# Loading the context tokens after the modulation weights in a two-block kernel, and turning their tiles between the first two products

## The chip, the core and the metric

The kernel runs on one core of one Trainium2 chip. The core has five engines with an instruction queue of their own: TensorE (PE, matrix products and transposes), VectorE (DVE), ScalarE (ACT), GpSimd (POOL) and SyncE (SP, which here issues every DMA). They run side by side and wait for each other through semaphores. The metric is the device time of one execution in microseconds, lower is better; the median of the runs is compared.

## What is computed

Two transformer blocks run on 512 latent tokens of width 1024. The first one also reads 256 context tokens. Only its beginning matters here:

```python
def modulate(h, g, shift, scale):
    return rmsnorm(h, g) * (1 + scale) + shift

sh_a, sc_a, g_a, sh_f, sc_f, g_f = modulation(c, ada_w[l], ada_b[l])              # silu(c) @ ada_w + ada_b
csh_a, csc_a, ... = modulation(c_ctx[None, :], ada_w[l], ada_b[l])
y_lat, y_ctx = token_mixer(modulate(x, norm1_g[l], sh_a, sc_a), modulate(h_ctx, norm1_g[l], csh_a, csc_a), w_in[l], ...)
```

`token_mixer` multiplies both sets of tokens by `w_in` and goes on with a gated recurrence in 8 heads, a convolution and attention. Then come a mixture of experts and the second block. All of it is in float32.

## The kernel before

Tokens stand along the free axis in the main buffers, so that the tokens, which arrive with 128 of them on the partitions, must first be turned. `HT` holds both kinds turned: columns 0 to 255 (`0:C`) are the context, columns 256 to 767 (`C:T`) the latent tokens, in KC = 8 chunks of 128 features. There are NT = 6 tiles of 128 tokens: t = 0 to 3 (LT = 4) are latent, t = 4 and 5 context.

**Start-up.** SP issues, in this order: the head of the constants, the four latent tiles, the context (L340, one transfer of 1 MB), 13 small rows of vectors (`rows1`), two of the eight units of modulation weights (phase `mod`, 1 MB each, of `ada_w`), 7 more rows (`rows2`), and the other six units. Then follow the eight units of `w_in` for head 0 (phase `hg`, 0.5 MB each), which lie over the places of modulation units 4 to 7, so that their issue waits until PE has used these. Behind them SP runs `sp_late_first` (L347 and on): the rest of the constants, then a wait for `turn_out` = 6 (all six tiles turned, since the token buffers are reused) and the first three "late" pieces.

ACT norms one tile after the other (`act_unit_tile`, four instructions and a half-row of small ones). PE turns each (L364, 8 transposes into two banks of PSUM, waits `x_unit`), DVE copies it to `HT` (L387). In `pe_setup` the turning of tiles 2 to 5 alternates with the products of modulation units 0 to 3 (L444); units 4 to 7 come after it. After unit 7, DVE copies the sums (L512), PE turns them (L504), and DVE makes shift and scale from them (L519, L527).

**The first norm.** `dve_first` (L633) applies shift and scale to the latent chunks (8 instructions 512 wide), then to the context's chunks (8 instructions 256 wide), and then builds `ht_sums` from the latent columns: for four pairs of chunks the sums and differences (L1881, L1883, L1885) that the seven-product scheme of later products wants.

**Head 0 on PE** (`pe_hg`): plain product 0 and plain product 1 over the latent tokens (L719, 8 chunks each, banks 0 and 1), the gates over the context (L745, bank 4), a wait for `ht_sums`, the product group 1 ("quad 1", L1863, 28 matrix products), values (L760), quad 2 (L1863), values, and the query (L768). The quads wait for `hq_out`, which says that DVE has taken the previous result out of the banks. A profile counts each of these float32 products twice.

**The late pieces on DVE** (`dve_hg`). The other two thirds of the modulation weights are multiplied on DVE in 32 pieces of 0.5 MB (L479, L481). Three buffers hold them; SP issues piece m when piece m - 3 is used (L469). DVE's order is: `dve_first`; `dve_hg_quad` 0 and the convolution (L825 to L832) which need plain products 0 and 1; pieces 0 to 8; quad 1 out of its banks (L1895 to L1902); pieces 9 to 17; quad 2 out of its banks; pieces 18 to 24; `dve_begin` (L861, L862), for which PE's first step of head 1 (L851) waits.

POOL forms sums of weights (`weight_sums`, L1870 to L1875), first when units 2 and 3 of `w_in` have arrived.

Of the kernel before, what the change touches and what calls it, by code (L numbers as in the profile page):

```python
# [13 lines left out]
KC = D // P  # L14
# [3 lines left out]
LT, CT_ = S // P, C // P  # L18
NT = T // P
# [81 lines left out]
def wait(eng, sem, n):  # L101

    if not (isinstance(n, int) and n <= 0):
        eng.wait_ge(sem, n)
# [83 lines left out]
def mixed_block_kernel(nc, A, out):  # L188

    ctx = ExitStack()  # L190
    with ctx:
        sems = {}

        def sem(name):
            if name not in sems:
                sems[name] = ctx.enter_context(nc.semaphore(name))
            return sems[name]
# [18 lines left out]
        psum = ctx.enter_context(nc.psum_tensor("psum", [P, 8, BANK], F32))  # L216
# [95 lines left out]
        def sp_rows(sp, rows, plan, full):  # L312

            r = n = 0
            for name, k in plan:
                if k == 0:
                    for half in range(2):
                        sp.dma_start(rows[r:r + 1, 64 * half:64 * half + 64], A[name]).then_inc(full, 16)
                        n += 1
                    r += 1  # L320
                    continue
                flat = A[name]
                if name in ("c_ctx", "final_norm_g", "final_norm_g_2"):
                    src = flat.rearrange("(r n) -> r n", n=P)
                elif name in ("conv_w", "conv_w_2"):
                    src = flat[0].rearrange("t (r n) -> (t r) n", n=P)
                else:
                    src = flat.rearrange("l (r n) -> (l r) n", n=P)
                sp.dma_start(rows[r:r + k, :], src).then_inc(full, 16)
                n += 1  # L330
                r += k
            return n
# [3 lines left out]
        def sp_setup(sp):  # L336
            sp.dma_start(consts[:, 0:CONST_HEAD], A["const_table"][:, 0:CONST_HEAD]).then_inc(sem("consts_in"), 16)
            for t in range(LT):
                sp.dma_start(x_tok[:, t, :], A["x"][0].rearrange("(t p) d -> t p d", p=P)[t]).then_inc(sem(f"x_in_{t}"), 16)
            sp.dma_start(c_tok, A["ctx"][0].rearrange("(t p) d -> p t d", p=P)).then_inc(sem("ctx_in"), 16)  # L340
            assert sp_rows(sp, rows1, ROWS1, sem("rows1_in")) == N_ROWS1

        def sp_setup_late(sp):
            assert sp_rows(sp, rows2, ROWS2, sem("rows2_in")) == N_ROWS2
# [9 lines left out]
                eng.wait_ge(sem("ctx_in"), 16)  # L354

        def turn_bank(n):
            return psum[:, 2 * (n % 2):2 * (n % 2) + 2, :].rearrange("p b n -> p (b n)")

        def pe_turn_tile(pe, t):

            pe.wait_ge(sem("x_unit"), t + 1)
            wait(pe, sem("turn_out"), t - 1)
            for k in range(KC):
                mm = pe.transpose(turn_bank(t)[:, k * P:(k + 1) * P], x_unit[:, t, k * P:(k + 1) * P], ident)  # L364
            mm.then_inc(sem("turned"), 1)

        def pe_setup(pe):
            pe.wait_ge(sem("consts_in"), 16)
            pe.wait_ge(sem("rows1_in"), 16 * N_ROWS1)
            pe.transpose(psum[:, 7, 0:123], rows1[0:123, :], ident[0:123, 0:123]).then_inc(once("rows1_turned"), 1)  # L370
            pe_turn_tile(pe, 0)
            pe_turn_tile(pe, 1)
            pe.wait_ge(sem("rows2_in"), 16 * N_ROWS2)
            pe.wait_ge(sem("vectors"), 1)
            pe.transpose(psum[:, 7, 128:128 + 92], rows2[0:92, :], ident[0:92, 0:92]).then_inc(once("rows_turned"), 1)
            for t in range(2, NT):
                pe_turn_tile(pe, t)
                pe_mod_first(pe, t - 2)
            for k in range(NT - 2, KC):
                pe_mod_first(pe, k)  # L380
            pe_mod_turn(pe, 0)

# [6 lines left out]
        def dve_setup(dve):  # L389
            dve.memset(psum[:, 4:7, :], 0.0)  # L390
            dve.drain()
            await_once(dve, "rows1_turned")
            dve.tensor_copy(vec1[:, 0:123], psum[:, 7, 0:123])
            dve.drain()
            dve.sem_inc(sem("vectors"), 1)
            dve_turn_tile(dve, 0)
            await_once(dve, "c_exp")
            dve.tensor_scalar(c_exp, c_exp, 1.0, None, ALU.add)
            dve.drain()
            dve.reciprocal(c_exp, c_exp)  # L400
            dve.drain()
            dve.tensor_tensor(silu_c.rearrange("p k w -> p w k"), c_exp.rearrange("p (w k) -> p w k", w=2),
                              vec1[:, CVEC:CVEC + 16].rearrange("p (w k) -> p w k", w=2), ALU.mult)\
               .then_inc(once("silu_c"), 1)
            dve_turn_tile(dve, 1)
            await_once(dve, "rows_turned")
            dve.tensor_copy(vec2[:, 0:92], psum[:, 7, 128:128 + 92]).then_inc(sem("vectors"), 1)
            for t in range(2, NT):
                dve_turn_tile(dve, t)

        def act_unit_tile(act, t):
# [217 lines left out]
        def dve_first(dve):  # L629

            for w, at_, end in ((0, C, T), (1, 0, C)):
                for k in range(KC):
                    dve.tensor_scalar(HT[:, k, at_:end], HT[:, k, at_:end], scale1[:, k, w:w + 1],  # L633
                                      mod[:, SH_A * KC + k, w:w + 1], ALU.mult, ALU.add).then_inc(sem("first_normed"), 1)
            dve.drain()
            for q in range(KC // 2):
                token_sums(dve, HT[:, 2 * q:2 * q + 2, C:T], ht_t[:, q])
            dve.sem_inc(once("ht_sums"), 1)
# [333 lines left out]
        def pe_hg(pe):  # L972

            pe_hg_plain(pe, 0)
            pe_hg_plain(pe, 1)
            pe_hg_gates(pe, 0, lambda: None)
            await_once(pe, "ht_sums")
            pe_hg_quad(pe, 0, 1, None)
            pe_hg_values(pe, 0, 0)
            pe_hg_quad(pe, 0, 2, None)  # L980
            pe_hg_values(pe, 0, 1)
            pe_hg_query(pe, 0)
            pe.wait_ge(sem("head_values_out"), 2)
            pe.wait_ge(sem("consts_in"), 32)
            pe_hg_head(pe, 1)
            pe_hg_head(pe, 2, True)
            with pe.Fori(3, HEADS) as i:
                pe_hg_head(pe, i)
# [2450 lines left out]
        PE_STEPS = [pe_setup, pe_hg, pe_tail, pe_attn, pe_merge, pe_router, pe_experts, pe_mix_norm, pe_in2, pe_dn, pe_wout2, pe_xproj, pe_xattn, pe_xo, pe_mlp, pe_last]  # L3439
        DVE_STEPS = [dve_setup, dve_mod, dve_first, dve_hg, dve_tail, dve_attn, dve_merge, dve_router, dve_experts, N(dve_norm, n_mix), dve_in2, dve_dn, dve_wout2, dve_norm_x, dve_xq, dve_xattn, dve_xo, dve_mlp, dve_last]  # L3440
        ACT_STEPS = [act_setup, act_hg, act_tail, act_attn, act_merge, act_router, act_experts, act_mix_norm, act_in2, act_dn, N(act_norm, n_mem), N(act_squares, n_x), act_xproj, act_xattn, act_xo, act_mlp, act_last_root, act_last]
        BETWEEN = {"mod": {1: sp_setup_late}, "hg": LATE_BETWEEN, "merge": {3: sp_x_again}, "experts": {SLOTS.index(0) - 1: sp_await_w_out}}
        SP_STEPS = [sp_setup] + [lambda e, n=n: ws.load(e, n, BETWEEN.get(n, {}), 3 if n == "hg" else 1) for n in ws.phases]
        SP_STEPS.insert(5, sp_router)
        SP_STEPS.insert(1 + 1 + 1 + list(ws.phases).index('pool2'), sp_small2)
# [56 lines left out]
```

## Time and profile before

| | us |
|---|---|
| median of 3 runs | 2726.17 |
| lowest, highest | 2725.04, 2728.87 |
| the profiled execution | 2727.93 |
| its span in the trace | 2726.2 |
| PE busy | 2648.6 |
| DVE busy | 1347.0 |
| ACT busy | 559.9 |

The trace covers the span; some 1.7 us of the execution lie outside it. PE is busy in 97% of the span, so what can be won lies in the few stretches where it stands. A digit of the profile's 40 slices stands for 68 us, and only the first slice shows PE well under full, with DMA at nine tenths. All times below are microseconds from the start of the span.

### The profile page before, as it was taken

To read this page: it belongs to the slowest core of one execution; us is meant where nothing else is said; L and a number is where in the kernel's file an instruction comes from. 1 tells how busy PE (TensorE), PEld (TensorE's weight loads), DVE (VectorE), ACT (ScalarE), POOL (GpSimd) and SP (SyncE) were. 2 spreads that over 40 slices of the span, in tenths; PEclk is the share of its full clock that TensorE was granted. 3 is DMA by queue.
4 is the path that set the end of the run, shared out by engine and by line. 5 is a ranking of instruction groups with operands and counts; after the bars stand their busy time and mean duration, and the time that the engine had idled before them with its cause. 6 is when DMAs were issued, how large, how long until landed. Compare 5 with 4: busy or idle time off the path is not lost.

```text
span 2726.2 us, 32908 instructions
## 1 busy us (share of the span) xinstructions
PE 2648.6 (97%) x12972; PEld 1868.0 (69%) x12972; DVE 1347.0 (49%) x2449; ACT 559.9 (21%) x942; POOL 177.3 (7%) x140
## 2 busy tenths in 40 slices
PE   6999999999999999998999999999999999999998
PEld 4788888888666666885433333334595877888887
DVE  5775566655555666545111111156472345654654
ACT  3122121222343343311111111132322112000001
POOL 1222221220000000231000000000000000000000
PEclk9999999999999999999999999999999999999999
DMA  9722221211112111336799999942003421323331
GB/s 337 224 81 59 55 58 42 62 31 39 47 55 55 50 52 47 93 94 240 284 409 409 409 409 409 409 126 70 24 1 93 139 62 47 92 79 93 87 84 47
DMA packets 332313, 374.79 MB, mean 137 GB/s; under 512 B 11329, under 2 KB 274326, under 8 KB 330902
## 3 DMA queue, kind: packets, MB, share of 16 engines
q1 hardware_dynamic: 331910, 371.93, 40.4%
q8 instruction: 90, 1.47, 0.2%
q10 hardware_dynamic: 272, 1.05, 0.1%
q14 instruction: 41, 0.34, 0.0%
HBM read 370.85 MB, written 2.10 MB: 137 GB/s over the span
## 4 chain that ended last, share of the span: by engine, by line
PE 89%; DVE 5%; DMA 3%; DVEq 1%; ACT 1%; issue 1%; SPq 0%; ACTq 0%
PE psum L1863 30%; PE psum L2250 12%; PE psum L1543 7%; PE psum L2428 5%; PE psum L760 3%; PE psum L1192 2%; PE psum L2107 2%; PE psum L2152 2%; PE psum L855 2%; PE psum L2966 2%; DMA arena<-in_ada_w 2%; PE psum L745 2%; PE psum L768 2%; PE psum L1399 2%; PE psum L1451 2%; PE psum L1428 2%
## 5 line engine op out<-in xcount | busy, mean ns | idle before, releaser
L1863 PE MATMUL psum<-arena 128*128 128x256 f32 x4144 | 908.0, 378 | 1.8 <-ACT arena L813 0.8
L1863 PEld LDWEIGHTS psum<-arena 128*128 128x128 f32 x4144 | 778.0, 189 | 119.0 <-issue 8.6
L2250 PE MATMUL psum<-arena 128*64 128x512 f32 x1536 | 349.5, 600 | 4.0 <-DMA arena<-in_w_down 2.4
L2250 PEld LDWEIGHTS psum<-arena 128*64 128x64 f32 x1536 | 103.7, 137 | 221.0 <-issue 217.3
L1543 PE MATMUL psum<-arena 128*128 128x256 f32 x896 | 206.6, 381 | 0.1
L1543 PEld LDWEIGHTS psum<-arena 128*128 128x128 f32 x896 | 164.7, 189 | 32.6 <-issue 11.4
L2157 DVE SCALAR_TENSOR_TENSOR arena<-psum,arena 128x512 f32<-128x512 f32 x64 | 48.1, 752 | 233.8 <-PE psum L2152 233.2
L2428 PE MATMUL psum<-arena 128*128 128x512 f32 (+1 forms) x416 | 157.0, 534 | 0.0
L1895 DVE TENSOR_TENSOR arena<-psum,arena 128x256 f32<-128x256 f32 x66 | 28.0, 425 | 260.8 <-ACT arena L1908 184.2
L2428 PEld LDWEIGHTS psum<-arena 128*128 128x128 f32 x416 | 79.7, 192 | 74.9 <-issue 70.6
L1870 POOL TENSOR_TENSOR arena<-arena 128x512 f32<-128x512 f32 x34 | 48.3, 1422 | 1058.2 <-DMA arena<-in_w_in 572.1
L1908 ACT ACTIVATE arena<-psum 128x256 f32<-128x256 f32 x32 | 12.3, 384 | 420.0 <-PE psum L1863 420.0
L760 PE MATMUL psum<-arena 128*128 128x128 f32 x768 | 88.3, 275 | 0.0
L760 PEld LDWEIGHTS psum<-arena 128*128 128x128 f32 x768 | 87.2, 192 | 0.1
L1416 ACT ACTIVATE arena<-psum,arena 128x768 f32<-128x768 f32 x64 | 57.4, 898 | 123.8 <-DVE arena L1410 123.7
L1192 PE MATMUL psum<-arena 128*128 128x512 f32 (+1 forms) x192 | 78.6, 560 | 0.0
L1408 DVE TENSOR_REDUCE arena<-psum 128x1 f32<-128x768 f32 x64 | 61.3, 958 | 23.9 <-PE psum L1399 22.5
L885 DVE TENSOR_TENSOR arena<-arena 128x768 f32<-128x768 f32 (+6 forms) x56 | 25.5, 454 | 95.9 <-PE psum L855 93.4
L2152 PE MATMUL psum<-arena 128*128 128x512 f32 x128 | 69.8, 633 | 0.0
L1438 ACT ACTIVATE arena<-psum 128x768 f32<-128x768 f32 x64 | 49.6, 812 | 98.0 <-PE psum L1428 97.1
L2107 PEld LDWEIGHTS psum<-arena 128*128 128x128 f32 x512 | 60.6, 198 | 12.8 <-issue 11.4
L782 ACT ACTIVATE arena<-psum 128x256 f32<-128x256 f32 x23 | 8.8, 384 | 292.2 <-PE psum L1863 292.2
(411 smaller groups left out, 3378.1 us busy)
## 6 DMA issues: line engine op xcount, KB each, us to landing
arena<-in_w_gate SPq DMA_DIRECT2D x64, 1024.0 KB, 18.5
arena<-in_w_up SPq DMA_DIRECT2D x64, 1024.0 KB, 18.4
arena<-in_w_down SPq DMA_DIRECT2D x64, 1024.0 KB, 18.5
arena<-in_w_in SPq DMA_DIRECT2D x120, 512.0 KB, 4.9
arena<-in_ada_w SPq DMA_DIRECT2D x32, 512.0 KB, 4.8
arena<-in_w_up SPq DMA_DIRECT2D x32, 512.0 KB, 5.4
arena<-in_w_down SPq DMA_DIRECT2D x32, 512.0 KB, 5.2
arena<-in_ada_w SPq DMA_DIRECT2D x8, 1024.0 KB, 13.0
```

The costliest lines, as they stand in the source:

```text
L745: mm = pe.matmul(psum[:, gates_bank(i), d * C:(d + 1) * C], ws.dst("hg", 4 + d)[:, k, :], HT[:, k, 0:C], start=(k == 0), stop=(k == KC - 1))
L760: mm = pe.matmul(psum[:, bank, t * P:(t + 1) * P], HT[:, k, tile * P:(tile + 1) * P], ws.dst("hg", 6)[:, k, :], start=(k == 0), stop=(k == ...
L768: mm = pe.matmul(psum[:, 0, :], ws.dst("hg", 7)[:, k, :], HT[:, k, C:T], start=(k == 0), stop=(k == KC - 1))
L1192: mm = pe.matmul(psum[:, item_bank(n), 0:item_cols(n)], ws.dst("attn", u)[:, k, :], x[:, k, :], start=(k == 0), stop=(k == KC - 1))
L1408: dve.tensor_reduce(a_stat[:, half, 0:1], score_banks(half), AX, ALU.max)
L1416: act.activation(a_prob[half], score_banks(half), ACT.Exp, bias=a_stat[:, half, 1:2], scale=SCALE, accum_out=a_stat[:, half, 2:3]).then_in ...
L1543: mm = pe.matmul(psum[:, 6 + phase % 2, at_ * HALF:(at_ + 1) * HALF], w, v, start=(at_ == 0 and j == 0), stop=(j == KC // 2 - 1), skip_gro ...
L1863: mm = pe.matmul(psum[:, base + b, c * HALF:(c + 1) * HALF], w, v, start=(first and q == 0 and m in (0, 2, 3, 4)), stop=(last and q == KC ...
L2107: mm = pe.matmul(psum[:, 6 + half, k * P:(k + 1) * P], h2tok[:, t, (4 * half + k) * P:(4 * half + k + 1) * P], hot[i % 2][:, t, :], start= ...
L2152: pe.matmul(psum[:, scatter_bank(i, n), :], ys[i % 2][:, n * P:(n + 1) * P], turned_hot[i % 2], start=True, stop=True)\
L2250: mm = pe.matmul(psum[64 * e:64 * e + 64, bank + n, :], tokens(e, 2 * q + k), w[:, k, 512 * n:512 * n + 512], start=(q == 0 and k == 0), s ...
L2428: mm = pe.matmul(psum[:, bank, 0:n], w[:, k, :], x[:, k, :], start=(k == 0), stop=(k == KC - 1))
```

## The change

SP leaves the context out of `sp_setup` and issues it behind the last modulation unit (`sp_context`, through `BETWEEN`). PE turns the two context tiles between plain product 0 and plain product 1, the first into banks 2 and 3, the second into banks 5 and 6. DVE copies them to `HT` after it has normed the latent chunks, and norms the context behind that. All six other places of PE's and DVE's order keep their sequence.

```diff
         def sp_setup(sp):
...
-            sp.dma_start(c_tok, A["ctx"][0].rearrange("(t p) d -> p t d", p=P)).then_inc(sem("ctx_in"), 16)
             assert sp_rows(sp, rows1, ROWS1, sem("rows1_in")) == N_ROWS1
+
+        def sp_context(sp):
+            sp.dma_start(c_tok, A["ctx"][0].rearrange("(t p) d -> p t d", p=P)).then_inc(sem("ctx_in"), 16)
...
         def turn_bank(n):
-            return psum[:, 2 * (n % 2):2 * (n % 2) + 2, :].rearrange("p b n -> p (b n)")
+            at_ = (0, 2, 0, 2, 2, 5)[n]
+            return psum[:, at_:at_ + 2, :].rearrange("p b n -> p (b n)")
...
             pe.wait_ge(sem("x_unit"), t + 1)
-            wait(pe, sem("turn_out"), t - 1)
+            wait(pe, sem("turn_out"), (0, 0, 1, 2, 4, 0)[t])
...
-            for t in range(2, NT):
+            for t in range(2, LT):
                 pe_turn_tile(pe, t)
                 pe_mod_first(pe, t - 2)
-            for k in range(NT - 2, KC):
+            for k in range(LT - 2, KC):
                 pe_mod_first(pe, k)
             pe_mod_turn(pe, 0)
...
-            for t in range(2, NT):
+            for t in range(2, LT):
                 dve_turn_tile(dve, t)
...
         def dve_first(dve):
 
             for w, at_, end in ((0, C, T), (1, 0, C)):
+                if w:
+                    for t in range(LT, NT):
+                        dve_turn_tile(dve, t)
+                    dve.drain()
...
         def pe_hg(pe):
 
             pe_hg_plain(pe, 0)
+            for t in range(LT, NT):
+                pe_turn_tile(pe, t)
             pe_hg_plain(pe, 1)
...
-        BETWEEN = {"mod": {1: sp_setup_late}, ...
+        BETWEEN = {"mod": {1: sp_setup_late, KC - 1: sp_context}, ...
```

PE's program before, from the second small transpose to the gates (the context tiles are the last two of the four groups of eight transposes at L364):

```order
L375 MATMUL psum<-arena 128x92
L364 MATMUL psum<-arena 128x128 x8
L444 MATMUL psum<-arena 2x512 x4
L364 MATMUL psum<-arena 128x128 x8
L444 MATMUL psum<-arena 2x512 x4
L364 MATMUL psum<-arena 128x128 x8
L444 MATMUL psum<-arena 2x512 x4
L364 MATMUL psum<-arena 128x128 x8
L444 MATMUL psum<-arena 2x512 x20
L504 MATMUL psum<-arena 128x128 x4
L719 MATMUL psum<-arena 128x512 x16
L745 MATMUL psum<-arena 128x256 x16
```

And now:

```order
L378 MATMUL psum<-arena 128x92
L367 MATMUL psum<-arena 128x128 x8
L447 MATMUL psum<-arena 2x512 x4
L367 MATMUL psum<-arena 128x128 x8
L447 MATMUL psum<-arena 2x512 x28
L507 MATMUL psum<-arena 128x128 x4
L726 MATMUL psum<-arena 128x512 x8
L367 MATMUL psum<-arena 128x128 x16
L726 MATMUL psum<-arena 128x512 x8
L752 MATMUL psum<-arena 128x256 x16
```

The 16 transposes of the context have moved from between the modulation products to between the two plain products.

DVE's program before, from the last tile copies to the first sums:

```order
L387 COPY arena<-psum 128x8x128 x4
L512 COPY arena<-psum 128x512
L519 TENSOR_TENSOR arena<-psum,arena 128x4x4 x2
L527 SCALAR_TENSOR_TENSOR arena<-arena 128x8 x2
L633 TENSOR_SCALAR arena<-arena 128x512 x8
L633 TENSOR_SCALAR arena<-arena 128x256 x8
L1881 TENSOR_TENSOR arena<-arena 128x512
```

And now:

```order
L390 COPY arena<-psum 128x8x128 x2
L515 COPY arena<-psum 128x512
L522 TENSOR_TENSOR arena<-psum,arena 128x4x4 x2
L530 SCALAR_TENSOR_TENSOR arena<-arena 128x8 x2
L640 TENSOR_SCALAR arena<-arena 128x512 x8
L390 COPY arena<-psum 128x8x128 x2
L640 TENSOR_SCALAR arena<-arena 128x256 x8
L1890 TENSOR_TENSOR arena<-arena 128x512
```

Two copies, which wait for PE, now stand between the latent norm and the context's, ahead of the sums.

## Rows read from the trace of the kernel before

**Rows 1.** The profile page, the chain that ended last, share of the span by engine
```profile
PE 89%; DVE 5%; DMA 3%; DVEq 1%; ACT 1%; issue 1%; SPq 0%; ACTq 0%
```

**Rows 2.** The same chain in order of time: start, length, what
```profile
13.86 19.99 DMA arena<-in_ada_w
...
38.30 15.98 PE psum L719 x32
...
54.91 0.50 ACT arena L780
55.54 0.69 DVE arena L825
...
59.38 4.16 DMA arena<-in_ada_w
...
112.02 1.29 DVE arena L481
...
114.51 1.16 PE psum L851 x8
```

**Rows 3.** Timeline of SP: start, length, what it issues
```profile
1.19 1.84 SPq L339 DMA_DIRECT2D arena<-in_x  x4
3.08 0.46 SPq L340 DMA_DIRECT2D arena<-in_ctx  x1
...
7.97 0.83 SPq L169 DMA_DIRECT2D arena<-in_ada_w  x2
```

**Rows 4.** Stretches: length, busy time of PE, PEld, DVE, ACT, POOL; clock, DMA share, GB/s
```profile
2.50:3.00 0.50, 0.00 (x0) 0.00 (x0) 0.00 (x0) 0.00 (x0) 0.00 (x0) 1.00 0.55 141
...
7.00:8.00 1.00, 0.00 (x0) 0.00 (x0) 0.00 (x0) 1.00 (x2) 0.00 (x0) 1.00 1.00 410
...
28.00:30.00 2.00, 2.00 (x24) 0.41 (x16) 1.08 (x1) 0.00 (x0) 0.00 (x0) 1.00 1.03 430
```

**Rows 5.** Timeline of PE: start, busy, line [idle before <- releaser]
```profile
19.84 1.04 PE L364 MATMUL psum<-arena 128*128 128x128 f32 x8
20.81 1.04 PE L444 MATMUL psum<-arena 128*2 128x512 f32 x8
...
31.35 1.04 PE L444 MATMUL psum<-arena 128*2 128x512 f32 x8 [0.85 <-DMA arena<-in_ada_w]
33.89 1.04 PE L444 MATMUL psum<-arena 128*2 128x512 f32 x8 [1.50 <-DMA arena<-in_ada_w]
```

**Rows 6.** Stretches again, granted clock around plain product 0
```profile
34.50:35.00 0.50, 0.43 (x5) 0.00 (x0) 0.00 (x1) 0.00 (x0) 0.00 (x0) 1.00 1.23 293
...
35.50:36.00 0.50, 0.26 (x1) 0.26 (x2) 0.19 (x1) 0.00 (x0) 0.00 (x0) 0.51 1.20 289
...
43.00:44.00 1.00, 1.00 (x4) 0.52 (x3) 1.00 (x1) 0.00 (x0) 1.00 (x1) 1.00 1.21 298
```

**Rows 7.** Timeline of DVE, PE and POOL, 16 to 56 us
```profile
27.86 1.23 DVE L387 COPY arena<-psum 128x1024 f32<-128x1024 f32 x1 [1.66 <-PE psum L364]
...
41.05 1.56 POOL L1870 TENSOR_TENSOR arena<-arena 128x512 f32<-128x512 f32 x1 [40.60 <-DMA arena<-in_w_in]
...
48.05 0.69 DVE L1881 TENSOR_TENSOR arena<-arena 128x512 f32<-128x512 f32 x1
...
53.68 0.59 PE L719 MATMUL psum<-arena 128*128 128x512 f32 x1
```

**Rows 8.** The norm: 256 wide, busy and mean ns; then both shapes, min/median/max ns
```profile
L633 DVE TENSOR_SCALAR arena<-arena 128x256 f32<-128x256 f32 x8 | 6.7, 907 | 0.0
...
L633 DVE TENSOR_SCALAR arena<-arena x16: 401/548/1518, 37.6 to 47.6; 128x512 f32<-128x512 f32 x8, 128x256 f32<-128x256 f32 x8
```

**Rows 9.** Timeline of PE, head 0 behind the gates
```profile
61.02 12.26 PE L1863 MATMUL psum<-arena 128*128 128x256 f32 x56
...
99.22 8.80 PE L768 MATMUL psum<-arena 128*128 128x512 f32 x16 [3.14 <-DVEq L1903]
...
114.51 1.16 PE L851 MATMUL psum<-arena 128*128 128x128 f32 x8 [2.44 <-DVEq L863]
```

More of the change, by code:

```diff
@@ L339, in sp_setup @@
                 sp.dma_start(x_tok[:, t, :], A["x"][0].rearrange("(t p) d -> t p d", p=P)[t]).then_inc(sem(f"x_in_{t}"), 16)
+            assert sp_rows(sp, rows1, ROWS1, sem("rows1_in")) == N_ROWS1
+        def sp_context(sp):
             sp.dma_start(c_tok, A["ctx"][0].rearrange("(t p) d -> p t d", p=P)).then_inc(sem("ctx_in"), 16)
-            assert sp_rows(sp, rows1, ROWS1, sem("rows1_in")) == N_ROWS1
         def sp_setup_late(sp):
@@ L3441, in mixed_block_kernel @@
         ACT_STEPS = [act_setup, act_hg, act_tail, act_attn, act_merge, act_router, act_experts, act_mix_norm, act_in2, act_dn, N(act_norm, n_mem), N(act_squares, n_x), act_xproj, act_xattn, act_xo, act_mlp, act_last_root, act_last]
-        BETWEEN = {"mod": {1: sp_setup_late}, "hg": LATE_BETWEEN, "merge": {3: sp_x_again}, "experts": {SLOTS.index(0) - 1: sp_await_w_out}}
+        BETWEEN = {"mod": {1: sp_setup_late, KC - 1: sp_context}, "hg": LATE_BETWEEN, "merge": {3: sp_x_again}, "experts": {SLOTS.index(0) - 1: sp_await_w_out}}
         SP_STEPS = [sp_setup] + [lambda e, n=n: ws.load(e, n, BETWEEN.get(n, {}), 3 if n == "hg" else 1) for n in ws.phases]
```

## The prediction

> **What bounds the kernel now.** I read the chain of work that ended last first. Over the whole span it is PE [rows 1], but in order of time its first 115 us are something else [rows 2]: a DMA of modulation weights until PE can take the last unit at 33.89, the norm and plain products 0 and 1, and from 55.54 on DVE and the DMAs of the late pieces, in turns, until 113.4, when `dve_begin` lets PE start head 1 at 114.51. In the timeline of PE this shows as waits of 3.14 and 2.44 us for DVE [rows 9]. So there are two clocks to watch. One is X, the start of plain product 0 (38.30 now). The other is D, the moment at which DVE enters the convolution and with it the late pieces (55.54 now). Since piece m is issued only when piece m - 3 is used, that stream is a closed loop between DVE and SP; a later D is a later head 1, and behind head 1 PE is busy almost without a gap. D is now set by ACT's copy of plain product 1 (54.91 + 0.50), while the sums on DVE end just ahead of it, at 55.2.
>
> **Modulation weights.** The removed transfer is 1.05 MB; the queue moves 430 GB/s in a full stretch [rows 4], so it is worth 2.4 us. Not all of it comes through. SP issues the first modulation unit at 7.97 [rows 3], or 7.5 without the context's 0.46. Its data would move at about 9.0, since the tiles issued at 1.19 to 3.0 only move from about 2.7 on (141 GB/s from 2.5 to 3.0 [rows 4]). The constants and four tiles, 2.2 MB, are through at about 8.1 by the sum of the rates up to there (410 GB/s from 7 to 8 [rows 4]). So the queue runs dry for 0.9 us, in which the 13 small rows find place that they take from the stream now; I count 0.7 lost. Unit 7 comes 1.7 us earlier, at 32.15. Bounds: 2.4 if nothing is lost, 0.5 if the first data come a microsecond later than I think.
>
> **The clock on unit 7.** Before, PE had the tile transposes between the modulation products (0.97 each, starts at 19.84 and 20.81 [rows 5]) and was at full clock until 35.0; then it fell to half, after a stretch in which it only took units 6 and 7, 2.5 us apart [rows 5, 6]. After the change nothing stands between units 3 to 7, and from about 25 us PE works 1.04 us of every 2.45. I take it that half clock (1.2 GHz) is granted before unit 7, so that its product takes 2.1 instead of 1.04: +1.0. Bounds 0 and +1.0. The transposes of the modulation run at half clock now too, so from there to X it stays 3.37 us (34.93 to 38.30). X = 32.15 + 2.1 + 3.4 = 37.6, against 38.30: 0.7 earlier. Unit 0 of `w_in` is there: unit 3 came at 41.05 [rows 7], 1.8 per unit at some 290 GB/s, so unit 0 came near 35.7; with as many bytes ahead of it and the dry 0.7 it comes at 36.4.
>
> The Trainium skill, page "TensorE: Matmul & The Clock Gate", section "HAM oscillation — how this bites in real kernels", speaks against the change here: small bursts of products with DMA waits between them let the gate fall back to half rate. The trace agrees at 35.5, where 0.51 stands in the row. By that rule the +1.0 stands, without it X would be 36.6.
>
> **PE.** The 16 transposes leave a stretch in which PE waited for DMA anyway, worth nothing there, and enter one where it did not: 2 x 0.97 = +1.94. Plain product 0 takes 8.93 (38.30 to 47.23, from the last product of the second at 53.68 less 15 of 0.43 each); it ran at half clock until about 42.1 [rows 6], and I leave that as it is. Product 1 then ends at X + 17.7, the gates at X + 24.65 = 62.2, against 61.02. ACT hides the norm of the context tiles: context lands near 34.6, two tiles of 2.9 us are done by 40.5, and PE wants them at 46.5.
>
> **DVE, the term that decides.** Before, the 256-wide norms took 6.7 us, 907 ns each, while the median over both widths is 548 [rows 8]. The slow ones ran beside POOL, which started at 41.05 [rows 7]; the shortest took 401. After, POOL is done near 47.5, before the context's norm begins at about 50, so I count 8 x 0.40 = 3.2. The wide norms end at about 41.4 and DVE then stands until PE has turned tile 4. From X: product 0 8.93, transposes of tile 4 0.97, the two copies 0.1 + 1.25 + 1.23 [rows 7], a drain 0.1, norms 3.2, a drain 0.1, sums 7.16 (48.05 [rows 7] to 55.21), 0.1: D = X + 23.1 = 60.7. Before it was X + 17.24. So the path grows by 5.9, X gives back 0.7, and D moves by +5.2. The sums end 1.5 us ahead of quad 1 (62.2), which so isn't held. The gates' columns are ready at X + 15.8, the gates begin at X + 17.7.
>
> The Trainium skill, page "SBUF — State Buffer", section "Who interferes with whom", says that VectorE instructions which read through the port pair shared with GpSimd wait for GpSimd's instruction, or it for theirs. The trace agrees: 907 beside POOL, 401 at the least. If the 907 belonged to the shape instead, the norm would cost 3.5 more and D move by 8.7.
>
> **What is queued behind.** SP stands in `sp_late_first` until tile 5 is copied, X + 12.5 = 50.1, and behind it wait the late pieces 0 to 2 (issued at 44.4 now) and two `w_in` units of head 1. These pieces are wanted at D + 3.05 = 63.8; they may take 13 us, and the rest of the constants keeps the queue full until about 53 anyway: nothing.
>
> **The late stream.** It starts 5.2 later. Piece 3 took 4.16 us to come [rows 2], behind a full queue; an empty one gives 3.7. POOL's second sums (61.35 to 67.9 now, which slowed pieces 4 and 5 to 2.0 from 1.29) move by only 1.2 and so now fall on pieces 0 to 2, which slows the issue of pieces 3 to 5 but spares 4 and 5. I count -0.5, bounds -1.7 and +0.5. Head 1 starts 4.7 later. PE meanwhile waits 3.4 us for quad 1 to be taken out of its banks (78.1 + 4.7 against 79.6), where it now waits hardly at all; that costs nothing, since D's stream and not PE sets head 1.
>
> **Sum.** -1.7 + 1.0 + 5.9 - 0.5 = +4.7 us on a span of 2726.2, which is the median too (the profiled execution's own time is 1.7 above it): 2726.2 + 4.7 = 2730.9, +0.17%. A measurement of this kernel can tell about 0.2%, 5.5 us, from no change, so this is just inside "the same".
>
> **Rivals.**
> 1. Half clock at the start of head 1. PE's wait before L851 was 2.44 us, and the clock held; the wait of 3.14 before L768 was followed by half clock, and the query took 8.80 instead of 6.87, 1.9 lost [rows 9]. After the change, PE finishes the query relatively earlier (it waits longer before quad 2 and less before the query, so the query may run at full clock), and the wait before L851 can be 2.6 to 4.5 us. From about 3 us on it decides: head 1 then starts at half clock, and as PE sets the end from there, 1.9 are added: 2730.9 + 1.9 = 2732.8, slower. Chance 0.34.
> 2. The stream takes most of it up: pieces come faster than I think, or full clock at unit 7 and nothing of the 2.4 us lost. X = 35.9, D +3.5, stream -1.7: +1.8, 2728.0. For it speaks that 4 to 5 us from issue to landing is most of a piece's round; against it, that nothing there is shortened by the change. Chance 0.17.
> 3. The context's transfer gets ahead or between the modulation units, or the queue runs dry for longer, so that X doesn't move: D +5.9, and with the stream +5.4, 2731.6 to 2732.5. Chance 0.05.
> 4. Faster. D doesn't decide and DVE's earlier free time is used: the whole 2.4 us reach head 1, 2723.8. Against it stands DVE's order, in which the pieces are behind the sums. Chance 0.02.
> My forecast has 0.42.
>
> **How the numbers follow.** The forecast spreads by 1.5 us either way around 2730.9 (the bounds of unit 7's clock and of the dry queue), so about three in ten of it lie beyond +5.5. Slower: 0.12 of the forecast, 0.30 of rival 1, 0.04 of rival 3: 0.46. Faster 0.02, the same 0.52. The range leaves out the lower half of rival 2, rival 4 and the upper edge of rival 1: 2727.8 to 2734.0.
>
> **What would show each step.** Unit 7's product (L447) should start near 32.2 and take 2.1 us; product 0 (L726) start near 37.6; the last copy of a tile (L390) end near 50.1; the context's norms (L640, 256 wide) take 0.4 us each; L832, the convolution's first instruction, start near 60.7 and wait for no one; L858 start near 119.2. If L832 starts below 58, the DVE term is wrong; if it does start near 60.7 and head 1 starts by less than 3 us later, the closed loop is wrong; if the end moves by more than head 1's start, it is the clock.

## The result and the profile after

The changed kernel takes 2736.99 us (median of 6 runs, 2732.05 to 2739.31), the kernel before 2727.22 (6 runs, 2725.04 to 2731.10); the ratio is 1.0029, 95% interval 1.0019 to 1.0039, that is 7.9 us (the two medians lie 9.8 us apart, which is within the interval). Measured again later on, beside 25 runs of before, it was 1.0023 (1.0013 to 1.0034). So the change makes the kernel slower by some 6 to 8 us, where +4.7 was forecast, and 2736.99 lies above the forecast range of 2727.8 to 2734.0. The first profiled execution took 2739.31 with a span of 2737.5; a second one, from the repeat, 2731.83 with 2730.0. In what follows X is the start of plain product 0, D DVE's entry into the convolution, H PE's first step of head 1 (L858, L851 before), and S its next step of the recurrence (L862, L855 before), 8 + 28 counted products later.

The chain that ended last, changed kernel, in order of time (start, length, what). It answers to [rows 2]:

```profile
26.00 12.10 DMA arena<-in_w_in
38.14 9.59 PE psum L726 x16
47.73 0.89 PE psum L367 x8
48.63 1.22 DVE arena L390
...
61.61 0.69 DVE arena L832
...
121.42 0.43 DVE arena L868
```

Before, the chain ran over both plain products and ACT's copy into the convolution. Now it leaves PE after product 0 and the first transposed context tile, and runs on DVE: copies, norm, sums, convolution. D is 61.61 and was 55.54.

The timeline of PE in the changed kernel (start, busy, line, idle before and its releaser). It answers to [rows 5, 9]:

```profile
32.39 1.89 PE L447 MATMUL psum<-arena 128*2 128x512 f32 x8 [0.64 <-DMA arena<-in_ada_w]
...
38.14 9.59 PE L726 MATMUL psum<-arena 128*128 128x512 f32 x16 [1.93 <-DMA arena<-in_w_in]
47.56 1.91 PE L367 MATMUL psum<-arena 128*128 128x128 f32 x16
...
85.01 15.23 PE L1872 MATMUL psum<-arena 128*128 128x256 f32 x56 [4.32 <-DVEq L1912]
...
106.71 7.11 PE L775 MATMUL psum<-arena 128*128 128x512 f32 x16 [1.11 <-DVEq L1912]
...
122.53 2.08 PE L858 MATMUL psum<-arena 128*128 128x128 f32 x8 [4.68 <-DVEq L870]
124.40 8.21 PE L1872 MATMUL psum<-arena 128*128 128x256 f32 x28
```

Three things are to be seen. Unit 7 starts at 32.39 and takes 1.89: it comes 1.5 us earlier and runs at half clock for most of it. Quad 2 waits 4.32 us for DVE and then takes 15.23 instead of 12.26. And head 1 begins after a wait of 4.68 us, at 122.53, and its first 36 products take 9.9 us, where they took 7.0 in the first trace of before (114.51 to 121.55).

The timeline of DVE, changed kernel. It answers to [rows 7, 8]:

```profile
36.97 3.74 DVE L640 TENSOR_SCALAR arena<-arena 128x512 f32<-128x512 f32 x8
48.63 2.36 DVE L390 COPY arena<-psum 128x1024 f32<-128x1024 f32 x2 [7.92 <-PE psum L367]
51.09 2.68 DVE L640 TENSOR_SCALAR arena<-arena 128x256 f32<-128x256 f32 x8
...
63.80 1.60 DVE L839 SCALAR_TENSOR_TENSOR arena<-arena 128x511 f32<-128x511 f32 x1
65.52 3.06 DVE L482 TENSOR_SCALAR arena<-arena 128x1024 f32<-128x1024 f32 x2
```

DVE has normed the latent chunks by 40.71 and then stands 7.9 us ahead of the copies. The context's norm takes 2.68 in place of 6.7. But the end of the convolution and the first two late pieces are stretched, 1.60 and 3.06 for 0.75 and 1.42 before.

**Where the 11.3 us between the first traces of the two kernels lie:** D +6.1 (55.54 to 61.61), D to H +1.9 (58.97 to 60.92), H to S +2.9 (7.04 to 9.92), the rest of the program +0.4. The second pair of traces has the same three, 4.6 us apart in span: D +3.6 (54.84 to 58.42), D to H +2.2 (58.88 to 61.05), H to S +1.1 (8.49 to 9.58), and -2.2 in all the rest. Over all 14 traces of this study what lies between S and the end of the span is 2601 to 2607 us. The two largest of these, 2607.2 and 2606.4, belong to the two kernels of the last experiment, in which work was moved into head 1; among the other twelve no relation to the edits is seen. So the change works in the first 132 us.

### The profile page after: what moved, and what is told of

Same layout as the page of the kernel before. It is cut to its first block, busy times and chain, and to the rows that moved or that the text cites. A ratio compares the mean times of both kernels' runs of the same rounds, so it can differ in the third digit from the quotient of the medians.

```text
span 2737.5 us, 32908 instructions
## 1 busy us (share of the span) xinstructions
PE 2656.4 (97%) x12972; PEld 1873.8 (68%) x12972; DVE 1345.0 (49%) x2449; ACT 560.3 (20%) x942; POOL 176.7 (6%) x140
## 3 DMA queue, kind: packets, MB, share of 16 engines
q8 instruction: 90, 1.47, 0.2%
## 4 chain that ended last, share of the span: by engine, by line
PE 88%; DVE 5%; DMA 3%; DVEq 1%; ACT 1%; issue 1%; SPq 0%; ACTq 0%
PE psum L1872 29%; PE psum L2259 12%; PE psum L1552 7%; PE psum L2437 5%; PE psum L767 3%; PE psum L1201 2%; PE psum L2116 2%; PE psum L2161 2%; PE psum L862 2%; PE psum L2975 2%; PE psum L752 2%; PE psum L775 2%; PE psum L1408 2%; DMA arena<-in_ada_w 2%; PE psum L1460 2%; PE psum L1437 1%
## 5 line engine op out<-in xcount | busy, mean ns | idle before, releaser
L1872 PE MATMUL psum<-arena 128*128 128x256 f32 x4144 | 912.8, 380 | 5.9 <-DVEq L1912 4.3
L1872 PEld LDWEIGHTS psum<-arena 128*128 128x128 f32 x4144 | 781.8, 190 | 124.2 <-issue 12.7
```

The source lines that it names most:

```text
L1872: mm = pe.matmul(psum[:, base + b, c * HALF:(c + 1) * HALF], w, v, start=(first and q == 0 and m in (0, 2, 3, 4)), stop=(last and q == KC ...
```

## The experiments

| kernel | X | D | H | S | D to H | H to S | median | ratio to before (95%) |
|---|---|---|---|---|---|---|---|---|
| before | 38.30 | 55.54 | 114.51 | 121.55 | 58.97 | 7.04 | 2727.22 | |
| before again | 37.62 | 54.84 | 113.72 | 122.21 | 58.88 | 8.49 | one run | |
| changed | 38.14 | 61.61 | 122.53 | 132.45 | 60.92 | 9.92 | 2736.99 | 1.0029 (1.0019, 1.0039) |
| changed again | 35.72 | 58.42 | 119.47 | 129.05 | 61.05 | 9.58 | 2734.17 | 1.0023 (1.0013, 1.0034) |
| order only | 37.92 | 58.92 | 118.79 | 128.60 | 59.87 | 9.81 | 2738.24 | 1.0037 (1.0023, 1.0051) |
| context behind w_in 1 | 35.06 | 56.76 | 117.97 | 126.68 | 61.21 | 8.71 | 2733.17 | 1.0024 (1.0015, 1.0033) |
| sums first | 36.34 | 55.83 | 116.11 | 123.16 | 60.28 | 7.05 | 2728.54 | 1.0002 (0.9993, 1.0011) |
| both of these | 36.73 | 55.67 | 115.00 | 123.65 | 59.33 | 8.65 | 2729.18 | 1.0001 (0.9992, 1.0010) |
| before, D delayed once | 37.59 | 56.58 | 118.48 | 128.41 | 61.90 | 9.93 | 2731.18 | 1.0014 (1.0005, 1.0022) |
| before, D delayed thrice | 37.97 | 60.47 | 121.94 | 131.27 | 61.47 | 9.33 | 2740.08 | 1.0049 (1.0036, 1.0062) |
| changed, PE filled | 36.34 | 60.15 | 121.07 | 128.12 | 60.92 | 7.05 | 2733.74 | 1.0023 (1.0014, 1.0031) |
| changed, POOL later | 35.87 | 58.95 | 120.03 | 129.66 | 61.08 | 9.63 | 2735.64 | 1.0026 (1.0017, 1.0035) |
| before, pieces spread | 37.60 | 54.80 | 112.56 | 119.50 | 57.76 | 6.94 | 2726.21 | 0.9991 (0.9982, 1.0000) |
| both, pieces spread | 36.26 | 56.30 | 112.64 | 119.58 | 56.34 | 6.94 | 2726.76 | 0.9998 (0.9989, 1.0007) |

X to S are those of one trace each, in us from the start of the span. Each ratio is against runs of the kernel before that were taken together with those of its row; 1.0010 is 2.7 us.

### Is it the order or the transfer?

The order alone, with the context's transfer in its old place:

```diff
+            sp.dma_start(c_tok, A["ctx"][0].rearrange("(t p) d -> p t d", p=P)).then_inc(sem("ctx_in"), 16)
             assert sp_rows(sp, rows1, ROWS1, sem("rows1_in")) == N_ROWS1
...
-        BETWEEN = {"mod": {1: sp_setup_late, KC - 1: sp_context}, ...
+        BETWEEN = {"mod": {1: sp_setup_late}, ...
```

> The new order on PE and DVE with the context's transfer back in its old place, ahead of the rows. Theory (the DVE path between the start X of plain product 0 and the start D of the convolution sets the loss): X is 38.3 as before, D is X + 23.5 = 61.8 as in the changed kernel (61.6), head 1's first step (L851 or L858) starts near 122 and the time is 2736 to 2738. Rival (the loss comes from the transfer behind the modulation weights, which leaves the queue dry at 36 us): most of it goes, the time is 2727 to 2730.

It costs about as much as the whole change: 1.0037 (1.0023 to 1.0051), an interval that overlaps with both of the changed kernel's. Timelines of PE and of DVE in it:

```profile
37.92 7.11 PE L725 MATMUL psum<-arena 128*128 128x512 f32 x16 [1.45 <-DVE arena L639]
44.86 1.91 PE L366 MATMUL psum<-arena 128*128 128x128 f32 x16
```

```profile
45.93 2.36 DVE L389 COPY arena<-psum 128x1024 f32<-128x1024 f32 x2 [4.97 <-PE psum L366]
...
58.92 0.69 DVE L831 TENSOR_TENSOR arena<-arena 128x512 f32<-128x512 f32 x1 [0.33 <-issue]
```

D is X + 21.0 here and not X + 23.5, since product 0 had full clock in this trace (7.11 against 9.59), and D and head 1 come some 3 us ahead of the expected 61.8 and 122. The theory stands in the times: the loss is the new order's. The transfer's move takes nothing back that can be measured.

The transfer, put behind two units of `w_in`:

```diff
-        BETWEEN = {"mod": {1: sp_setup_late, KC - 1: sp_context}, ...
+        BETWEEN = {"mod": {1: sp_setup_late}, ...
...
-        LATE_BETWEEN = {7: sp_late_first, ...
+        LATE_BETWEEN = {1: sp_context, 7: sp_late_first, ...
```

> The changed kernel with the context's transfer behind units 0 and 1 of w_in instead of ahead of them. Theory: unit 0 of w_in no longer waits behind 1 MB, X falls from 38.1 to about 36.9 (the modulation chain's own end), D to 60.4, and since the late stream follows D the time falls by 1 to 1.5 us against the changed kernel. Rival (the queue's dry stretch is what costs, through everything behind it): X stays at 38 or the late stream starts earlier by 3 us or more.

X 35.06, earlier than expected; D 56.76; yet H is 117.97, and the ratio is 1.0024 (1.0015 to 1.0033), between the changed kernel's two. A gain of a microsecond or so isn't excluded and isn't shown. Of the expected X the reason is only half right. In the second trace of the changed kernel unit 7 came at 31.04 and X was 35.72 with no wait for `w_in` at all. What held X at 38.14 in the first trace can be read there from SP's issues and from the stretches (length, busy PE, PEld, DVE, ACT, POOL, clock, DMA share, GB/s):

```profile
26.42 4.99 SPq L169 DMA_DIRECT2D arena<-in_w_in  x1
...
31.45 4.79 SPq L169 DMA_DIRECT2D arena<-in_w_in  x1
```

```profile
34.00:35.00 1.00, 0.28 (x4) 0.00 (x0) 0.66 (x1) 0.00 (x0) 0.00 (x0) 0.50 1.17 298
...
36.00:37.00 1.00, 0.21 (x1) 0.00 (x0) 0.55 (x5) 0.52 (x1) 0.00 (x0) 0.50 0.14 40
```

Single issues of `w_in` took 4.99 and 4.79 us on SP's queue, and just behind them the DMA engines ran dry, 40 GB/s in one microsecond. In the second trace the same stretch shows 291 GB/s. But the long issues alone don't make the hole: in that second trace, too, one issue of `w_in` took 4.77 us (at 25.09) and the next 3.52. The hole cost little of X. Without it product 0 would have begun 0.69 us after DVE's first norm at 36.97, as it does in the second trace (35.03, 35.72), that is at 37.66: 0.5 us earlier. The rest of the 2.4 us between the two X is unit 7, which started 1.35 earlier in the second trace, and the clock of unit 7 and of the transposes behind it (0.6). What sets the hole off stays open.

### Is it DVE's path to D?

The sums of the latent columns moved ahead of the context's copies and norm, into the time in which DVE stood:

```diff
                 if w:
+                    dve.drain()
+                    for q in range(KC // 2):
+                        token_sums(dve, HT[:, 2 * q:2 * q + 2, C:T], ht_t[:, q])
+                    dve.sem_inc(once("ht_sums"), 1)
                     for t in range(LT, NT):
                         dve_turn_tile(dve, t)
                     dve.drain()
...
             dve.drain()
-            for q in range(KC // 2):
-                token_sums(dve, HT[:, 2 * q:2 * q + 2, C:T], ht_t[:, q])
-            dve.sem_inc(once("ht_sums"), 1)
```

> The changed kernel with DVE's sums of the latent columns (7.2 us) ahead of the two context copies and the context's norm, in the 7.9 us in which DVE now stands. Theory: D is no longer set by the sums but by ACT's copy of plain product 1, X + 19 = 57.1 (61.6 in the changed kernel); head 1 starts 4 to 5 us earlier than there, and the time is 2730 to 2733. Rival (D doesn't matter, the late stream is bound by DMA or by POOL): under 1 us gained against the changed kernel.

The loss is gone: 1.0002 (0.9993 to 1.0011). The timelines of DVE and then of PE in its trace:

```profile
50.05 2.36 DVE L390 COPY arena<-psum 128x1024 f32<-128x1024 f32 x2
52.50 2.67 DVE L644 TENSOR_SCALAR arena<-arena 128x256 f32<-128x256 f32 x8
55.83 0.69 DVE L833 TENSOR_TENSOR arena<-arena 128x512 f32<-128x512 f32 x1 [0.66 <-ACT arena L788]
```

```profile
100.97 9.71 PE L776 MATMUL psum<-arena 128*128 128x512 f32 x16 [4.19 <-DVEq L1913]
...
116.11 1.16 PE L859 MATMUL psum<-arena 128*128 128x128 f32 x8 [1.38 <-DVEq L871]
```

DVE now waits 0.66 us for ACT's copy of product 1, as expected, and D is 55.83. It is the one edit that decides between the theories: the transposes are still between the plain products and the transfer is still late, and the time is that of before. The result was better than expected (2730 to 2733 for the time, against a median of 2728.54; D 57.1), in part by luck: X came early, the long wait of PE came before the query, whose half clock (9.71) is hidden, and head 1 began at full clock. Even so the time is that of before, and not below it.

Both edits together:

> Both: sums first on DVE, context's transfer behind units 0 and 1 of w_in. Theory: X 36.9, D X + 19 = 55.9, head 1 starts at about 115, time 2726 to 2729, level with the kernel before. Rival: as the single edits, no sum of the two.

1.0001 (0.9992 to 1.0010), level with before as the theory said, with X, D and H (36.73, 55.67, 115.00) where it put them, and no sum of two gains. In its timeline of PE the wait stands at head 1 again:

```profile
99.20 7.11 PE L776 MATMUL psum<-arena 128*128 128x512 f32 x16 [3.14 <-DVEq L1913]
...
115.00 2.07 PE L859 MATMUL psum<-arena 128*128 128x128 f32 x8 [4.66 <-DVEq L871]
```

### What does a later D cost by itself?

The kernel before, with n = 1 or n = 3 repeats of one pair's sums on DVE (they write the same values again):

```diff
             for q in range(KC // 2):
                 token_sums(dve, HT[:, 2 * q:2 * q + 2, C:T], ht_t[:, q])
+            for _ in range(n):
+                token_sums(dve, HT[:, 0:2, C:T], ht_t[:, 0])
             dve.sem_inc(once("ht_sums"), 1)
```

> The kernel before with one pair's latent sums formed once more on DVE ahead of the ht_sums signal (3 instructions, 1.8 us), so that D, the start of the convolution, is later and nothing else is changed. Theory (closed loop: head 1 follows D, and the end follows head 1): D 57.3 instead of 55.5, head 1 at 116.3, time +1 to +3 us against before. Rival (the stream has slack for it): within 0.5 us of before.

> The same with three repeats (9 instructions, 5.3 us). Theory: D 60.9, near the changed kernel's 61.6; POOL's weight sums from 61.3 on lie on the convolution and the first pieces as they do there, so head 1 starts 6 to 8 us later than before, and if its first matrix products are granted half clock (wait before L851 over 3.5 us) the time is 7 to 11 us over before, about that of the changed kernel: the whole loss without any of its edits. Rival (the loss is in the transfer or in PE's order): under 5 us over before.

1.8 us more on DVE cost 1.0014 (1.0005 to 1.0022), 3.8 us; 5.3 us cost 1.0049 (1.0036 to 1.0062), 13.3 us by the ratio. Both are more than expected (1 to 3 us, 7 to 11 us), and the second is more than the changed kernel loses. None of the change's edits is in these kernels. The timelines of PE, in the one with a single repeat and then in the one with three:

```profile
118.48 2.08 PE L853 MATMUL psum<-arena 128*128 128x128 f32 x8 [4.57 <-DVEq L865]
```

```profile
85.51 14.11 PE L1865 MATMUL psum<-arena 128*128 128x256 f32 x56 [7.29 <-DVEq L1905]
...
121.94 2.08 PE L853 MATMUL psum<-arena 128*128 128x128 f32 x8 [4.52 <-DVEq L865]
```

With three repeats D is 4.9 later than in the first trace of before, H 7.4 and S 9.7. With one repeat it is 1.0 for D (X was 0.7 earlier in that trace), 4.0 for H and 6.9 for S. So D to H grew by 2.5 us with the long delay and by 2.9 with the short one: the stream adds about the same to either, and not a multiple of the delay. Behind it both pay for half clock at head 1 (H to S 9.33 and 9.93). In the times the two doses cost 2.1 and 2.5 times their length, with wide intervals (1.4 to 6.0 us and 9.8 to 16.9 us). That the long delay costs more than itself is shown; a factor is not. Even the S of three repeats doesn't reach 13.3; the rest of that trace is 2606 us, inside the spread of the others, and the ratio's lower end is 9.8.

### The two amplifiers

PE's wait at head 1, filled with five products into an unused bank (all results stay the same):

```diff
             if l == 0:
+                if isinstance(i, int) and i == 1:
+                    for _ in range(5):
+                        pe.matmul(psum[:, 7, :], ones, HT[:, 0, C:T], start=True, stop=True)
                 pe.wait_ge(sem("head_begun"), i)
```

> The changed kernel with five matrix products of 512 columns (0.86 us each at full clock, 4.3 us) into the unused bank 7 just ahead of PE's wait for head 1's start, so that PE doesn't stand there for 4.7 us. Theory (half clock at the start of head 1 costs 2.9 us of the 10.9): L858 and the 14 products behind it take 1.1 and 6.2 instead of 2.1 and 8.2, and the time falls by 2 to 3 us against the changed kernel. Rival: clock unchanged, time the same or up.

The timeline of PE in this kernel, head 1's first products (L861 and L1875 here, L858 and L1872 in the changed kernel):

```profile
121.07 1.16 PE L861 MATMUL psum<-arena 128*128 128x128 f32 x8 [0.18 <-DVEq L873]
122.07 6.21 PE L1875 MATMUL psum<-arena 128*128 128x256 f32 x28
```

In the trace it did what it should: 0.18 us of waiting left, H to S 7.05 for 9.6 and 9.9. That much of the clock is shown. In the times it is not: 1.0023 (1.0014 to 1.0031) lies inside both intervals of the changed kernel. The expected gain of 2 to 3 us is 0.0007 to 0.0011 of the time, which such intervals neither show nor exclude.

Over all traces, waits at H of 0 to 2.44 us are followed by full clock (H to S 6.9 to 7.05, five traces), and waits of 4.3 to 5.2 us by half clock for part of it (8.5 to 9.9, nine traces). Before again is one of the latter: it waited 4.34 at L851 and paid 1.4. The kernel before thus already pays for this in one of its two traces, and the change adds less to it on the whole than the first pair of traces says.

POOL's second sums held until late piece 2 is used:

```diff
                 pool.wait_ge(sem("head_gates"), i + 1)
+                if is_first(i):
+                    pool.wait_ge(sem("late_used"), 3)
```

> The changed kernel with POOL's second weight sums of head 0 held until late piece 2 is used. Theory (POOL's instructions beside the convolution's end and pieces 0 to 2 stretch them by 3.1 us in sum and delay the issue of piece 3): L839 takes 0.75 instead of 1.60, the first two pieces 1.4 instead of 3.1, piece 3 is issued 2.5 us earlier, head 1 starts 1 to 2.5 us earlier and the time falls with it. Rival (the slowed pieces are hidden behind DMA either way): head 1 moves by less than 0.5 us.

The timeline of DVE in this kernel (the convolution's last instruction is L841 here, L839 in the changed kernel), with the first late pieces behind it:

```profile
61.13 0.75 DVE L841 SCALAR_TENSOR_TENSOR arena<-arena 128x511 f32<-128x511 f32 x1
62.00 1.42 DVE L482 TENSOR_SCALAR arena<-arena 128x1024 f32<-128x1024 f32 x2
63.51 1.28 DVE L484 SCALAR_TENSOR_TENSOR arena<-arena 128x1024 f32<-128x1024 f32 x1
```

The stretched instructions are back at their old lengths, so POOL did stretch them. But D to H is 61.08, no shorter, and the ratio is 1.0026 (1.0017 to 1.0035): the rival holds. The collision is hidden in the wait for piece 3 (3.02 us in this trace) or given back later: up to the emptying of quad 1 the stream takes 20.3 us from D, against 20.6 and 20.7, and these tenths are gone again by H. So the 2 us by which D to H has grown (60.9 to 61.9 in seven of the eight traces with a late D, 59.9 in the eighth; 58.9 and 59.0 in the two of before) don't come from it. They are spread: in the two pairs of traces the first third of the stream (to the emptying of quad 1) is longer by 0.7 and 1.1, the second by 0.7 and 0.5, the last by 0.5 and 0.6. Sums first, whose D (55.83) is hardly later than before's, takes 60.3 from D to H all the same, so that a late D can't be all of it. Their cause stays open.

### Taking pieces off the stream

If the stream ahead of H sets the end, fewer pieces ahead of it should help, in the kernel before too:

```diff
-            dve_late(dve, 18, 25)
+            dve_late(dve, 18, 22)
...
-            dve_hg_head(dve, 1, {"quad_2": ...
+            dve_hg_head(dve, 1, {"quad_0": lambda dve: dve_late(dve, 22, 23), "conv_1": lambda dve: dve_late(dve, 23, 24),
+                                 "conv_2": lambda dve: dve_late(dve, 24, 25), "quad_2": ...
...
-                        13: lambda sp: sp_late(sp, 21, 28), 21: ...
+                        13: lambda sp: sp_late(sp, 21, 25), 15: lambda sp: sp_late(sp, 25, 28), 21: ...
```

> The kernel before, with three of the seven late pieces that stand ahead of head 1's start (22, 23, 24) moved on DVE behind it, one each behind quad 0 and the two halves of the convolution of head 1, and SP's issues of pieces 25 to 27 two weight units later. Theory (the late stream ahead of head 1's start sets the end): dve_begin comes 5 to 6 us earlier, so that PE no longer waits for DVE at L851 (2.4 us); the time falls by 2 us against before, less if DVE now holds up PE inside head 1. Rival: DVE is late inside head 1 by as much, time the same or more.

> The same three pieces moved in the kernel with sums first and the context's transfer behind units 0 and 1 of w_in, which was level with before. Its PE waits 4.7 us at head 1's start and pays some 1.6 us of half clock there. Theory: both go, the time falls by 4 to 6 us against before, a kernel faster than both. Rival: as e9, the wait moves into head 1.

The timeline of PE in the first of the two, head 1's first step and a later one:

```profile
112.56 1.05 PE L851 MATMUL psum<-arena 128*128 128x128 f32 x8
...
143.45 1.23 PE L855 MATMUL psum<-arena 128*128 128x128 f32 x8 [1.54 <-DVEq L900]
```

`dve_begin` starts 4.0 us earlier than in the first trace of before (109.35 for 113.39), not 5 to 6. PE no longer waits at H, and DVE holds it up by 1.54 us inside head 1 instead of 0.16. The time is 0.9991 (0.9982 to 1.0000) of before, the lowest ratio of all kernels here, with an interval that just touches no change, so that a gain isn't shown. On the improved version of the change the same edit gives 0.9998 (0.9989 to 1.0007), not the 4 to 6 us expected; PE waits 1.72 us inside head 1 there, as the rival said in part.

The second traces:

> The kernel before once more, for a second trace. If the intervals repeat, D is 55.5 and head 1 starts 59.0 later, at full clock; if the stretch between D and head 1 differs by more than 1 us, differences of that size between single traces say nothing of an edit.

> The changed kernel once more, for a second trace and times on this chip. D about 61, head 1 61 us later, its first 36 small products at half clock; X between 36 and 38, since other kernels with the same early order showed 36.3 and 35.9 where the first trace had 38.1. Time 6 to 10 us over before.

The timeline of PE in the second trace of before, then of the changed kernel:

```profile
98.23 7.11 PE L768 MATMUL psum<-arena 128*128 128x512 f32 x16 [3.14 <-DVEq L1903]
...
113.72 2.07 PE L851 MATMUL psum<-arena 128*128 128x128 f32 x8 [4.34 <-DVEq L863]
```

```profile
31.04 1.76 PE L447 MATMUL psum<-arena 128*2 128x512 f32 x8 [0.61 <-DMA arena<-in_ada_w]
...
35.72 8.80 PE L726 MATMUL psum<-arena 128*128 128x512 f32 x16 [1.44 <-DVE arena L640]
...
119.47 2.08 PE L858 MATMUL psum<-arena 128*128 128x128 f32 x8 [4.91 <-DVEq L870]
```

D to H repeats within 0.13 us in both kernels, so that the 2 us between them are no accident of one trace. X, D and the clock at H don't repeat: X differs by 2.4 and D by 3.2 us between the two traces of the changed kernel, H to S by 1.4 between those of before. Both expectations missed there: full clock at head 1 in before, and D of about 61 in the changed kernel.

## Why the prediction was wrong

**Right: what bounds the kernel.** The two moments X and D, and that the way from D to head 1 is DVE's and the late pieces', are borne out by the repeats on DVE and by sums first. What that way takes once D is late was forecast wrongly (below).

**Right: DVE, the term that decides.** It was put at D = X + 23.1, +5.2 in all. Measured: X + 23.5 and X + 22.7, so that the path grew by 6.2 and 5.5 us where 5.9 was forecast. D moved by +6.1 and +3.6, +4.8 on the mean; that this is near 5.2 owes something to chance, since X moved by -0.2 and -1.9 where -0.7 was forecast. Of its parts, the norm took 2.68 for 3.2, and from the first sum to D it was 7.75 for 7.26, with 0.5 us of standing in it. The page "SBUF — State Buffer" of the Trainium skill, section "Who interferes with whom", was rightly read: away from POOL the 256-wide norm is 0.33 us each, beside POOL it was 0.91 [rows 8], and the convolution's last instruction doubled when POOL came upon it.

**Right about modulation weights, with too narrow a bound.** Unit 7 was put at 32.15, between 31.5 and 33.4; it started at 32.39 and at 31.04, the second 2.85 earlier than in [rows 5], more than the 2.4 of the transfer. Unit 0 of `w_in` was put at 36.4, out of the way; in the first trace PE waited for it until 38.14, which made X 0.5 us later than DVE's norm alone would have.

**Right, with a scatter that was not foreseen: the clock on unit 7.** 1.89 and 1.76 us, half clock for most of it. As the Trainium skill has it under "HAM oscillation — how this bites in real kernels" in "TensorE: Matmul & The Clock Gate", bursts between DMA waits let the clock fall; the first trace of the changed kernel agrees, 0.50 from 30 to 38 us. The waits in the page's example are longer than the 1.45 us here, so for these the traces alone speak, and they don't all say the same: in the kernel with POOL later, units 6 and 7 started at 28.47 and 30.98 with waits of 1.24 and 1.47, and both took 1.04 us at full clock. And product 0, taken as unchanged at 8.93, took from 7.1 to 10.2 us over these kernels.

**Wrong in size, the step that failed: the late stream.** It stood at -0.5 with bounds of -1.7 and +0.5. It was +1.9 and +2.2, outside them, and +2.9 and +2.5 where only D was delayed. I had argued from POOL's sums, which would spare pieces 4 and 5, and from an empty queue for piece 3. Holding POOL back left D to H as it was (61.08), and the loss lies in every third of the stream, while I had only reasoned about the first six pieces of 25. Why the stream takes longer when D is late stays open.

**Wrong in choice: half clock at head 1.** This was rival 1 with 0.34, and it is what happened, in both traces: the wait before H was 4.68 and 4.91, just above the 2.6 to 4.5 named. Its mechanism was right too, down to the query at full clock after a short wait. It should have been the forecast: with D's stream later by 4 us and PE's own work unchanged, PE must wait longer somewhere, and the last wait, ahead of H, is the one that isn't hidden. Its price of 1.9 was taken from the query in one trace of before (8.80 less 6.87; at full clock the query measured 7.11, so 1.7). Head 1's first products paid 2.9 and 1.1 more than in the two traces of before. The sign named for it, an end that moves by more than head 1's start, holds in the first pair (11.3 against 8.0 us) and not in the second (4.6 against 5.8). That this clock costs time in the medians isn't shown: filling the wait took it away in the trace and not measurably in the times.

**Sum.** 4.8 (D) + 2.1 (stream) + 2.0 (clock) = 8.9 on the mean of the two pairs, less 0.9 in the rest, is 8.0 us, against 7.9 and 6.3 by the two ratios. The forecast had 5.2 - 0.5 + 0 = 4.7. Mechanism and place were right; of the three terms the stream was too small by 2.6 us and the clock at head 1 by 2.0, both to the same side. Another 1.0 us of the distance between 2730.9 and 2736.99 is the kernel before itself, which was taken at 2726.2 and measured 2727.22 in six runs.

## What to carry to other kernels

When a step is moved behind a wait on another engine, look at what stands behind it on its own engine: here 7 us of sums that needed nothing of what they now waited for, while the engine stood for 7.9 us. Moving these ahead made the change free. Don't take the cost of a late start from a look at the first rounds of a loop of load and use: here such a loop took 2 to 3 us longer in seven of the eight traces with a late start, and the experiment with a delay of known length showed it without any other edit. And when one engine is later by some microseconds, the other's wait must go somewhere: find the last wait that is not hidden, and ask what the clock was behind waits of that length.

## What the runs showed of the hardware

- A DMA issue held SyncE's queue for 4.99 us while the queue moved 414 GB/s (26 to 28 us), and a second one for 4.79; the DMA engines ran nearly dry at the end of the second (40 GB/s from 36 to 37 us). In another execution of the same kernel one issue took 4.77 us, and the engines moved 291 GB/s from 36 to 37 us.
- In the changed kernel, products of 1.04 us with waits of 1.45 between them were followed by half clock (1.00 up to 28 us, 0.86 from 28 to 30, 0.50 from 30 on). In the kernel with POOL later, products of the same length behind waits of 1.24 and 1.47 kept full clock (1.00 up to 33 us).
- Two executions of one kernel differ in where half clock falls: the query after the same wait of 3.14 us took 8.80 in one trace of before and 7.11 in the other. Head 1's first products took 7.04 us after a wait of 2.44 in the one and 8.49 after a wait of 4.34 in the other.
